# A chunk's third product ahead of the inverse's second product, and VectorE's state update ahead of the inverse's add, in a fused transformer kernel

## The reference, cut to what matters

```python
def wkv7_scan(r, w, k, v, a, b):
    """S_t = S_{t-1} diag(w_t) + (S_{t-1} a_t) b_t^T + v_t k_t^T ; y_t = S_t r_t."""
    def step(state, inp):
        r_t, w_t, k_t, v_t, a_t, b_t = inp
        sa = jnp.einsum('bhvk,bhk->bhv', state, a_t)
        state = (state * w_t[:, :, None, :] + sa[..., None] * b_t[:, :, None, :]
                 + v_t[..., None] * k_t[:, :, None, :])
        return state, jnp.einsum('bhvk,bhk->bhv', state, r_t)
    _, ys = lax.scan(step, s0, xs)
```

## Time and profile before

| what | value |
|---|---|
| median of 3 runs | 3466.57 us (3465.11 to 3469.8) |
| profiled execution: own time | 3465.34 us |
| profiled execution: span | 3463.4 us |
| TensorE busy over the span | 3247.9 us (94%) |
| VectorE busy | 2009.3 us (58%) |
| ScalarE busy | 1055.9 us (30%) |
| GpSimd busy | 1674.6 us (48%) |
| mean granted TensorE clock | 0.978 of full speed |

### The profile page before, as it was taken

One profiled execution on the slowest core, in us unless ns is written; L12 is line 12 of the kernel. 1 busy time (PEld: TensorE's weight loads), 2 busy tenths in 40 slices (PEclk: granted clock), 3 DMA queues, 4 the chain that ended last, 5 costly groups with the idle time before them and its releaser, 6 DMA issues.

```text
span 3463.4 us, 52617 instructions
## 1 busy us (share of the span) xinstructions
PE 3247.9 (94%) x19342; PEld 2566.8 (74%) x19342; DVE 2009.3 (58%) x2727; ACT 1055.9 (30%) x1970; POOL 1674.6 (48%) x1323
## 2 busy tenths in 40 slices
PE   7988999899999999899999999999989899999999
PEld 4756777777888887576777788877657677788887
DVE  5647677765566545624645666656552635586556
ACT  2142333322121113543534321112551535231112
POOL 3423322225476664244344666655226263576665
PEclk9998999999999999999999999999999999999999
DMA  5431111112232221012121232222112121222222
GB/s 206 165 121 44 44 38 38 38 38 67 91 100 96 95 95 61 31 55 67 54 69 62 85 98 92 97 86 80 36 37 92 37 86 44 85 90 93 97 96 92
DMA packets 71657, 268.36 MB, mean 77 GB/s; under 512 B 7840, under 2 KB 7968, under 8 KB 68384
## 3 DMA queue, kind: packets, MB, share of 16 engines
q1 hardware_dynamic: 69152, 260.73, 22.6%
q10 hardware_dynamic: 2304, 4.83, 0.4%
HBM read 263.44 MB, written 2.10 MB: 77 GB/s over the span
## 4 chain that ended last, share of the span: by engine, by line
PE 75%; DVE 16%; ACT 5%; issue 2%; DMA 1%; POOL 0%; DVEq 0%; SPq 0%; ACTq 0%; POOLq 0%
PE psum_a L574 10%; PE psum_a L578 10%; PE psum_a L577 10%; PE psum_d L637 5%; PE psum_d L574 5%; PE psum_d L577 5%; PE psum_d L578 5%; PE psum_a L729 3%; PE psum_d L832 2%; PE psum_a L600 2%; PE psum_a L603 2%; PE psum_a L604 2%; PE psum_a L759 1%; PE psum_a L763 1%; PE psum_a L762 1%
## 5 line engine op out<-in xcount | busy, mean ns | idle before, releaser
L3297 POOL TENSOR_TENSOR w_lo<-raw,w_hi 128x1024 fp32r<-128x1024 f32 x440 | 1114.3, 2532 | 36.7
L3293 POOL TENSOR_TENSOR mark<-mark 128x1 f32<-128x1 f32 x438 | 105.5, 241 | 1712.7 <-PE psum_a L574 866.7
L574 PE MATMUL psum_a<-h_hi,w_hi 128*128 128x512 f32 x1712 | 676.7, 395 | 0.0
L578 PE MATMUL psum_a<-h_hi,w_lo 128*128 128x512 f32 x1712 | 669.1, 391 | 0.0
L577 PE MATMUL psum_a<-h_lo,w_hi 128*128 128x512 f32 x1712 | 668.9, 391 | 0.0
L3294 POOL TENSOR_SCALAR w_hi<-raw 128x1024 fp32r<-128x1024 f32 x440 | 471.2, 1071 | 33.8 <-DMA raw<-in_weights 33.8
L574 PEld LDWEIGHTS psum_a<-h_hi,w_hi 128*128 128x128 f32 x1712 | 323.1, 189 | 78.1 <-issue 11.2
L577 PEld LDWEIGHTS psum_a<-h_lo,w_hi 128*128 128x128 f32 x1712 | 323.1, 189 | 68.0 <-issue 1.9
L578 PEld LDWEIGHTS psum_a<-h_hi,w_lo 128*128 128x128 f32 x1712 | 322.7, 189 | 68.0
L574 PE MATMUL psum_d<-split,w_hi 128*128 128x512 f32 x848 | 331.1, 390 | 9.5 <-DVE x L3044 6.7
L577 PE MATMUL psum_d<-split,w_hi 128*128 128x512 f32 x848 | 330.0, 389 | 0.0
(11 more groups left out here) (394 smaller groups left out, 5713.9 us busy)
## 6 DMA issues: line engine op xcount, KB each, us to landing
raw<-in_weights SPq DMA_DIRECT2D x440, 512.0 KB, 3.4
plain<-in_ada SPq DMA_DIRECT2D x20, 1024.0 KB, 7.2
arena<-in_ada SPq DMA_DIRECT2D x4, 1024.0 KB, 17.5
x<-in_x SPq DMA_DIRECT2D x1, 2048.0 KB, 12.8
x<-in_x ACTq DMA_DIRECT2D x1, 2048.0 KB, 10.7
out<-x SPq DMA_DIRECT2D x8, 256.0 KB, 3.7
arena<-in_pe ACTq DMA_DIRECT2D x2, 512.0 KB, 3.6
const<-in_const ACTq DMA_DIRECT2D x1, 906.0 KB, 9.4
```

The source lines that it names most:

```text
L574: m = pe.eng.matmul(dst, wh, hi(t), start=t == 0, stop=False)
L578: m = pe.eng.matmul(dst, wl, hi(t), start=False, stop=t == k - 1)
L3293: eng.tensor_tensor(b.mark[:, 1:2], b.mark[:, 0:1], b.mark[:, 0:1], ALU.add)
L3297: eng.tensor_tensor(lo, b.raw[:, s], hi.bitcast(F32), ALU.subtract).then_inc(sig["w_ready"], 1)
```

## The change

On TensorE, `chain.third(c)` moves from behind the inverse's second product to ahead of it, right behind `chain.second(c)`. On VectorE, `dve_rwkv_state` moves from behind the two adds of the inverse to ahead of them. As the tiles of `psum_d` are taken in another order, both moves belong together. The order in `psum_a` stays the same, and ScalarE, GpSimd and SyncE have the same instructions in the same order. No instruction is added or removed.

```diff
@@ pe_rwkv
         if c is not None:
             chain.second(c)
+            chain.third(c)
         pe.eng.wait_ge(inverse.free, pe.taken(inverse))
         pe.eng.wait_ge(z.free, pe.taken(z))
         normal = products(lambda *at: block(b.R_TW, *at), lambda *at: block(b.R_Z, *at))
@@
             pe_rwkv_maps(pe, j, (0, 1))
-        if c is not None:
-            chain.third(c)
         if k == 3 and more:
             pe_rwkv_length(pe)
@@ dve_rwkv
         if k == 5:
             if j:
                 dve_rwkv_centered(v)
+        if j and k < NQ:
+            dve_rwkv_state(v, j - 1, k - 1)
         for half in range(2):
             dst = every(b.R_TN, half)
@@
         if k == 5:
             dve_rwkv_maps(v, (0, 1))
-        if j and k < NQ:
-            dve_rwkv_state(v, j - 1, k - 1)
         if k in (1, 3) and more:
             dve_rwkv_input(v, j + 1, k)
```

## The result

The changed kernel takes 3489.07 us (median of 4 runs, 3488.55 to 3492.35), the kernel before 3465.84 us in the same comparison: a ratio of 1.0069, with a 95% interval of 1.0052 to 1.0087. The profiled execution took 3492.35 us, the longest of the four, with a span of 3490.4 us, 27.0 us more than before.

The account below looks back on a forecast made before the run. TensorE was taken to set the pace in the rounds. Rounds 1 to 4 cost 8.1, 11.8, 4.6 and 5.4 us, together 29.9, on the median 3496.5, said as 3495 us; range 3484 to 3507.

Parts of the forecast that it names:

- What bounds the rounds: Pair 2's rounds: TensorE, busy 39.37 of 44 us, sets the pace; the old order hides two waits in each other's work.
- The terms of rounds 1 to 3: From `second` to the next first product: 4.00, 4.73 and 4.23 us, costing 1.55, 1.74 and 0.50 us per round.
- the gain that I had allowed for late adds: Round 2: in two pairs the adds were already about 0.2 us late, taking 0.4 us off the cost in all.
- Round 4: Each pair costs the larger of 0.30 us and 1.74 us less TensorE's old wait for VectorE; together 5.4 us.
- The term of 0.30 us for VectorE: Round 4: VectorE's path grows by 0.30 us, the least cost in pairs where it was already behind.
- Pair 7's gain: Pair 7, round 1: `third` fills TensorE's 1.54 us wait for VectorE's late masks, a gain of 1.2 us.
- all of it passes on: The whole 29.9 us reaches the total, because every later step of a pair waits for the last round on both engines.
- the wait for the state: VectorE's state update, at most 1.15 us, ends ahead of the adds and does not hold them; counted as nothing.
- Part taken up in round 4: Rival: where VectorE was behind, a later TensorE waits 9.6 us less, giving about 3486 us; chance 0.09.
- The clock falls in the new gaps: Rival: TensorE's clock drops in the added waits, 29 us on top in 21 rounds, about 3524 us; chance 0.08.
- Faster: Rival: VectorE's masks are late, so `third` fills waits for them, giving 3452 us; chance 0.04.
- No change: Rival: the waits for U that go and those for the adds that come cancel; chance 0.04.

Follow-up runs that it names:

- e1: Changed kernel with only the third product's new-state matmuls ahead of the inverse's second product, its output matmuls back behind it: 3483.14 us, 1.0048 of the kernel before.
- e4: Changed kernel with round 3's short product L637 also moved ahead of the inverse's second product: 3502.04 us, 1.0104 of the kernel before.
- e3: Kernel before with the third product moved ahead of the inverse's second product in round 4 alone: 3473.40 us, ratio 1.0018.
- e5: Kernel before with `chain.first` ahead of the inverse's transpose on TensorE, and W's copy ahead of the transpose's copy on ScalarE: 3458.54 us, ratio 0.9974.
- e2: Kernel before with only the third product's output matmuls ahead of the inverse's second product, VectorE's order as before: 3489.07 us, ratio 1.0069.

## Why the prediction was right

**What bounds the rounds** was right: TensorE's path, with two waits that each held the other's work. e1's round 1 shows that what goes back into the adds' wait is gained in full, e4 that what is taken out of it costs its length.

**The terms of rounds 1 to 3.** The new length of each round was right to 0.02 us in all seven pairs, pair 7's round 2 too (2.76 + 1.74 = 4.50). In round 2 of pairs 3 and 6 the gain that I had allowed for late adds, 0.2 us each, was 0.25 and 0.3. The terms came from rows of the same kernel: U's copy and its release, `third`'s length, and pair 0 as the picture of the adds' wait with nothing in it. The 1.05 us of pair 0 came back 19 times among the 22 waits for the adds.

**Round 4** was right in form: e3 confirms it pair by pair. In pair 1, where TensorE's path decides, the cost was 0.26 us (forecast 0.33). The term of 0.30 us for VectorE in pairs 2, 4 and 5 measured 0.01, -0.01 and 0.16. VectorE's masks were late by those 0.30 us (1.30 us after the round's first product instead of 1.01), but a later instruction stretched less. Pair 4, VectorE's L2448 and GpSimd's instruction beside it (GpSimd splits weights there), first before, then the same two in the changed kernel:

```profile
573.27 2.47 DVE L2448 SCALAR_TENSOR_TENSOR arena<-arena,par 128x512 f32<-128x512 f32 x1
572.82 2.36 POOL L3297 TENSOR_TENSOR w_lo<-raw,w_hi 128x1024 fp32r<-128x1024 f32 x1
```

```profile
589.16 2.16 DVE L2447 SCALAR_TENSOR_TENSOR arena<-arena,par 128x512 f32<-128x512 f32 x1
588.42 2.35 POOL L3296 TENSOR_TENSOR w_lo<-raw,w_hi 128x1024 fp32r<-128x1024 f32 x1
```

L2448, 0.75 us long where GpSimd is idle, ends 0.56 us after GpSimd's end in the one and 0.55 in the other, though it began 0.29 us later in its round. GpSimd's end kept its place, 9.4 us after the round's first product. So VectorE's lateness was taken up by a wait that the profile shows as a longer instruction. I had left such changes to the range.

**Pair 7's gain** was 1.47 us, not 1.2, and by the mechanism named: the masks were late again, and `third` filled the wait. VectorE's masks, and TensorE's second product right behind both, in the changed kernel's pair 7, round 1:

```profile
766.58 0.95 DVE L2546 TENSOR_TENSOR arena<-psum_d,const 128x256 f32<-128x256 f32 x2
```

```profile
767.69 0.69 PE L1192 MATMUL psum_d<-arena,plain 64*64 64x64 f32 x32
```

The masks end at 767.53, `third` holds TensorE from 766.45 to 767.69, and no idle time is left between. The clock stayed up, for which I had taken off some 0.2 (by my own terms `third` ends at 743.81 + 0.44 + 1.23 = 745.48, a gain of 1.4).

**The step that fell short** is "all of it passes on". The sum, 29.9, was 1.6 too high in the stretches (28.2): 0.9 in round 4, 0.3 in pair 7's gain, 0.3 from the wait for the state in pair 2, which I counted for nothing, and 0.1 in round 2. Between the pairs 2.2 us came back, in two places where the clock had fallen before and now stayed up. The larger, 1.6 us, lies behind pair 4, where from the first to the second product of round 5 it was 3.45 us before and 2.08 now. TensorE's idle time ahead of them had been cut from 2.09 to 1.45 us, but that alone does not decide it. With the same 1.45 us the clock fell in e3, and with 2.08 us it stayed up in e5. The first and second product of round 5, pair 4, in e3 and in e5:

```profile
580.10 1.13 PE L1192 MATMUL psum_d<-arena 64*64 64x64 f32 x32 [1.45 <-DVE arena L2564]
583.90 1.13 PE L1192 MATMUL psum_d<-arena,plain 64*64 64x64 f32 x32
```

```profile
576.00 0.69 PE L1192 MATMUL psum_d<-arena 64*64 64x64 f32 x32 [2.08 <-DVE arena L2562]
578.07 0.69 PE L1192 MATMUL psum_d<-arena,plain 64*64 64x64 f32 x32
```

So these 2.2 us were luck as far as the runs show, and I had foreseen the clock only as a loss. The median lies 3.3 us below the profiled execution. The mean granted clock of that execution was 0.979, of the three faster ones 0.981; where they gained has no trace.

**The rivals.** "Part taken up in round 4" would have been 3486. The measured 3489 lies between it and the forecast, but it was not that: pairs 2, 4 and 5 kept their round 4, and e1 shows that a delay ahead of the masks is not taken up. "The clock falls in the new gaps": not in the profile of the changed kernel, which has 0.979 overall; but e1, e3 and e4 show that it can, from waits that the changed kernel has too. That the forecast escaped it is in part luck: pair 0's row, on which I relied, is one place of many. My text called the price a multiple of the sum; by the rival's own rows it is about once the sum, 29 us, if every round paid. "Faster": no wait for masks appeared. "No change": both waits grew.

## What to carry to other kernels

When two engines wait for each other in turn, write down for each wait what stands in it. A piece of work moved out of one wait costs its length there, or the wait's, whichever is shorter, and gains only what it covers where it arrives; here both places lost. A part of the same kernel without the piece, such as a first iteration, measures the bare wait and is the best row for a forecast. And where a late engine seems to give slack, ask from which instruction on it is late: a delay that comes in ahead of that passes whole.

## What the runs showed of the hardware that was not expected

TensorE's granted clock fell to 0.50 after idle times of 0.66 and 0.37 us within two, in e4 and e1, at a place where the same two waits in the other pairs left it at 1.00. It cost 2.5 us each time in e4 and 1.0 in e1. In the earlier trace rows the fall had come only after a further idle time of 1.54 us; the 0.57 in the earlier trace rows is the mean of a stretch in which it fell, and from 745.3 to 748.7 it was 0.50. The Trainium skill ("TensorE: Matmul & The Clock Gate", "A second HAM failure mode: psum-queue depth-cycling") says of bf16 matmuls of 512 columns that cycle through PSUM banks that frequent micro-idle times between groups make the clock swing. Here the matmuls are f32 and 64 to 128 columns wide; e4's trace agrees in round 1 of 2 of its 7 pairs (5.1 us of 35.3), the changed kernel's in none. Which pairs it strikes changes from kernel to kernel; what decides that stays open.

Several of VectorE's instructions that read `arena` alone took longer while GpSimd split weights (L3297). L2448, 0.75 us long by itself, took 2.47 us where it overlapped that instruction for 1.92 us, 1.79 with 1.25 and 1.06 with 0.51; L2452, 0.69 us by itself, took 2.72 with 2.17. Each ended about 0.55 us after GpSimd's end. The reciprocal L2446, which reads `arena` too, took 3.35 us in every pair, with 0 to 3.3 us of GpSimd's work beside it, and the products L2520 and L2523, which also read `psum_d`, kept their 0.69 us beside it. So where such an instruction sets the pace, a change of some tenths of a microsecond in when it starts can cost 2 us or nothing, as in e2's pair 3 and in pair 4 above.
